# Reordering one stage of a hybrid decoder layer: page numbers read early, a norm moved, a softmax cut in two

## The chip, the core and the metric

The kernel runs on one core of one Trainium2 chip. TensorE (PE) multiplies matrices, VectorE (DVE), ScalarE (ACT) and GpSimd (POOL) work on elements, and SyncE (SP) here issues transfers only; GpSimd issues transfers too. The metric is the device time of one execution in microseconds, as the median of several runs. Less is better.

## The reference, cut to what matters

One layer is computed for a prompt group (512 tokens) and a sample group (8 sequences of 4 new tokens): a mixer of four parts side by side, then cross-attention to a memory, then a SwiGLU FFN. All weights are float32. The change touches three of the mixer's four parts.

```python
# sample attention over a paged cache: 8 sequences, 16 pages of 128 rows each
k_past = k_cache[layer, page_table].reshape(db, past, H, dh)
gate = jnp.einsum('bqhd,bnhd->bhqn', q, kmean)
_, idx = lax.top_k(gate, n_sel)                       # 3 of 8 blocks
p = jax.nn.softmax(sc, axis=-1)
o = jnp.einsum('bhqnk,bhqnkd->bhqd', p_sel, vs) + jnp.einsum('bhqk,bkhd->bhqd', p_own, own_v)
# Mamba-2 ("ssm"): chunked scan, then a gate and one norm over its 256 columns
return rms_norm(y * jax.nn.silu(z), norm_w), conv1, h1
# HGRN2 ("hgrn"): decays between any two tokens of a chunk
diff = bcum[:, :, None] - bcum[:, None, :]
att = jnp.einsum('blhk,bshk,blshk->blsh', qc, kc, dec)     # dec = exp(diff), masked
o = att applied to v, plus q * exp(bcum) times the state;  S = decayed S + k^T v
```

## The kernel before, in words

A core runs the layer as stages: inputs, the input projection (`win`), `ssm` (which also holds `hgrn`), `gdn`, and four more for the output projection, the cross-attention and the FFN. Every stage ends when TensorE, VectorE and ScalarE have all passed its end. Within a stage each engine has its own instruction list; semaphores tie them together.

The change lies in the `ssm` stage. There four pieces of work are interleaved by hand. Each is a Python generator per engine, and the string `LANES` (L2893) says whose turn it is: "m" is the main chain (`ssm_*`, then `hgrn_*`), "p" the sample attention over pages (`moba_sample_*`), "u" the L2 norms and products that prepare the next stage (`unit_*`), and "n" the norm of Mamba-2's output (`ssm_norm_*`). The same string drives all three engines, so one letter moved changes the order on each of them. Instructions of one engine run in that order; a wait holds all that stands behind it.

The main chain. When Mamba-2's states are made, VectorE gates its output `Y`, writes the squares into `xdt` and signals `tail_sq` (L1947 to L1952). `ssm_norm_tensor` (L1844) sums the squares of each half of the tokens with two matmuls into bank 4, `ssm_norm_scalar` takes the root of each half (L1968), and `ssm_norm_vector` takes the reciprocal of the 128x544 tile (L1959) and scales `Y` (L1961). HGRN2 computes its decays by halving levels, j = 1 to 7: `diff(j)` on VectorE (two subtractions into `h_d`), `exps(j)` on ScalarE (L2384), `scaled(j)` on VectorE (queries and keys times the decays), matmuls of level j on TensorE (`hgrn_tensor`), and `place(j)` on VectorE, which copies the scores of levels 0 to 4, and at the end those of 5 to 7 together, out of four rotating PSUM banks (L2303). TensorE can't reuse a bank before its scores are placed. Level j+2 is prepared while level j is multiplied. Then follow `tail_decay_vector` and the product `kd`, and with them the tail: five tiles of 128, 128, 128, 128 and 32 tokens, each with a turn step (transposes) and a product step, the last with many small matmuls for the samples.

The pages. 32 quarters (numbers 0 to 31) of keys and 32 of values (32 to 63) pass through four slots. Each quarter is four transfers of 128 KB; SP issues the even quarters, GpSimd the odd ones. The page numbers lie in a table in SBUF, so each transfer needs a number in a register (`value_load`, L439). `load_pages` reads a quarter's four numbers, waits until its slot is free, and issues its four transfers:

```python
for n in quarters:
    ...
    ids = [eng.value_load(PTAB[...]) for i in range(4)]
    m_ = n - NPG
    if 0 <= m_ < 32:
        eng.wait_ge(S("satt_turned"), 2 * m_ + 2)
    elif m_ >= 32:
        eng.wait_ge(S("ms_values_used"), m_ - 31)
```

Each number is read when the issuing queue comes to its quarter, and not before. The first four quarters of values take the slots of the last keys. Then comes the softmax: the choice of blocks ends on VectorE at L1517, nine exponentials with row sums follow on ScalarE in one step (L1553, L1554), TensorE turns the probabilities in five groups, ScalarE copies them out, and `own pv` (new tokens' values) and then `pv32` to `pv63` (one per quarter of values, four matmuls each) run on TensorE. When `pv63` is done VectorE scales the result into `ms_o` (L1525, L1526), and TensorE picks each head's rows.

Of the kernel before, what the change touches and what calls it, by code (L numbers as in the profile page):

```python
# [23 lines left out]
P = 128  # L24
# [43 lines left out]
def build(nc, a, o):  # L68
# [12 lines left out]
    with ctx:  # L81
# [226 lines left out]
        mp_stat = m(3, 16)  # L308

        NPG = 4  # L310
        pages = carve(WS, 0, NPG, 4, 2 * P)
        ms_s = carve(WS, NPG * 4 * 2 * P, PAST)
        ms_bias = carve(XN, 0, PAST + NS)
# [117 lines left out]
        def pages_sem(n):  # L431

            return S(f"pages{n % NPG}_in"), 64 * (n // NPG + 1)

        def load_pages(eng, quarters):
            for n in quarters:
                cache = a["cache_moba_k"] if n < 32 else a["cache_moba_v"]
                pg, e = divmod(n % 32, 2)
                ids = [eng.value_load(PTAB[0:1, (2 * i + e) * NPAGE + pg:(2 * i + e) * NPAGE + pg + 1], min_val=0,  # L439
                                      max_val=a["cache_moba_k"].shape[1] - 1) for i in range(4)]  # L440
                m_ = n - NPG
                if 0 <= m_ < 32:
                    eng.wait_ge(S("satt_turned"), 2 * m_ + 2)
                elif m_ >= 32:
                    eng.wait_ge(S("ms_values_used"), m_ - 31)
                else:
                    after(eng, "win")
                for i in range(4):
                    eng.dma_start(pages[:, n % NPG, i, :],  # L449
                                  cache[0].rearrange("g p h d -> g p (h d)")[bass.ds(ids[i], 1)].rearrange("g p n -> (g p) n"))\  # L450
                       .then_inc(pages_sem(n)[0], 16)
# [932 lines left out]
        def moba_sample_tensor(pe):  # L1384
# [28 lines left out]
            for j in range(66):  # L1413
# [2 lines left out]
                if j < 64:  # L1416
                    turn(j)
                yield
            for _ in range(4):
                yield  # L1420
            pe.wait_ge(S("satt_exp"), 1)
            for i in range(4):
# [65 lines left out]
        def moba_sample_vector(v):  # L1488
            moba_queries_vector(v)
            yield  # L1490
            s3 = ms_s.rearrange("p (n k) -> p n k", k=MOBA_BLOCK)
            for j in range(69):
                q, x = (j - 2) // 16 - 1, (j - 2) % 16
                if j == 8:
                    moba_rows_vector(v)
                if q >= 0 and x == 0:
                    v.wait_ge(S("ms_scores_out"), q + 2)
                    link(V.tensor_reduce(ms_gate[:, 2 * q:2 * q + 2], s3[:, 2 * q:2 * q + 2, :], AXX, ALU.add))
                elif q >= 0 and x == 1:
                    sl = slice(q * 512, (q + 1) * 512)  # L1500
                    link(V.scalar_tensor_tensor(ms_s[:, sl], ms_bias[:, sl], mr, ms_s[:, sl], ALU.mult, ALU.add))
                elif q >= 0 and x == 2:
                    link(V.tensor_reduce(ms_top[:, 2 * q:2 * q + 2], s3[:, 2 * q:2 * q + 2, :], AXX, ALU.max))
                yield
            gm = bc(ms_gate.rearrange("p (o m) -> p o m", o=1), (P, 8, 8))
            gn = bc(ms_gate.rearrange("p (n o) -> p n o", o=1), (P, 8, 8))
            link(tt(ms_gt, gm, gn, ALU.is_gt))
            link(tt(ms_eq, gm, gn, ALU.is_equal))
            link(tt(ms_eq, ms_eq, ltm, ALU.mult))
            link(tt(ms_gt, ms_gt, ms_eq, ALU.add))  # L1510
            link(V.tensor_reduce(ms_rank, ms_gt, AXX, ALU.add))
            link(V.tensor_scalar(ms_sel, ms_rank, 2.5, NEG, ALU.is_gt, ALU.mult))
            link(tt(ms_top, ms_top, ms_sel, ALU.add))
            link(V.tensor_reduce(ms_stat[:, 0:1], ms_top, AXX, ALU.max))
            link(V.tensor_reduce(ms_stat[:, 1:2], ms_own, AXX, ALU.max))
            link(V.tensor_reduce(ms_stat[:, 2:3], ms_stat[:, 0:2], AXX, ALU.max, negate=True))
            V.tensor_scalar(ms_shift, ms_sel, ms_stat[:, 2:3], None, ALU.add).then_inc(S("satt_max"), 1)  # L1517
            yield
            for _ in range(5 + 32):
                yield  # L1520
            v.wait_ge(S("satt_exp"), 1)
            link(V.tensor_reduce(ms_stat[:, 0:1], ms_sums, AXX, ALU.add))
            link(V.reciprocal(ms_stat[:, 3:4], ms_stat[:, 0:1]))
            v.wait_ge(S("ms_values_used"), 32)
            link(V.tensor_scalar(ms_o[:, 0, :], bank(7)[:, 0:GW], ms_stat[:, 3:4], None, ALU.mult))  # L1525
            V.tensor_scalar(ms_o[:, 1, :], bank(7)[:, GW:2 * GW], ms_stat[:, 3:4], None, ALU.mult).then_inc(S("satt_o"), 1)  # L1526
            yield
            yield
            v.wait_ge(S("satt_pv"), 1)
            V.tensor_copy(OM[:, 0:2, SEQ:T], bank(5)[:, 0:2 * NS].rearrange("p (c t) -> p c t", t=NS))  # L1530
            yield

        def moba_sample_scalar(s):
# [17 lines left out]
            for n in range(8):  # L1551
                sl = slice(n * MOBA_BLOCK, (n + 1) * MOBA_BLOCK)
                A.activation(ms_s[:, sl], ms_s[:, sl], ACT.Exp, bias=ms_shift[:, n:n + 1], accum_out=ms_sums[:, n:n + 1])  # L1553
            A.activation(ms_own, ms_own, ACT.Exp, bias=ms_stat[:, 2:3], accum_out=ms_sums[:, 8:9]).then_inc(S("satt_exp"), 1)  # L1554
            yield
            for i in range(4):
# [286 lines left out]

        def ssm_norm_tensor(pe):  # L1844
            pe.wait_ge(S("tail_sq"), 1)
            for j in range(2):
                if j:
                    pe.wait_ge(S("tail_root"), 1)
                for k in range(2):
                    last = mm(bank(4)[:, 0:HT], ones, half(xdt[:, k, :], j), k == 0, k == 1)  # L1850
                last.then_inc(S("tail_sum"), 1)
                yield
            yield
# [10 lines left out]
        def ssm_vector(v):  # L1864
# [84 lines left out]
                link(V.scalar_tensor_tensor(Y[:, c_, :], xc[:, c_, :], par(R_SD + c_), Y[:, c_, :], ALU.mult, ALU.add))  # L1949
            link(tt(Y, Y, proj[:, C_Z:C_Z + 2, :], ALU.mult))  # L1950
            tt(xdt, Y, Y, ALU.mult).then_inc(S("tail_sq"), 1)
            yield  # L1952

        def ssm_norm_vector(v):
# [10 lines left out]
        def ssm_norm_scalar(s):  # L1965
            for j in range(2):
                s.wait_ge(S("tail_sum"), j + 1)
                A.activation(half(rsq, j), bank(4)[:, 0:HT], ACT.Sqrt, bias=eps, scale=1.0 / GW).then_inc(S("tail_root"), 1)  # L1968
                yield
            yield  # L1970

        def ssm_scalar(s):
            def decays(i):
# [37 lines left out]
            s.dma_start(o["ssm_p"][0, 0].rearrange("(c e) q n -> (e q) c n", e=2), s_fin).then_inc(S("ssm_states_out"), 16)  # L2011
            s.wait_ge(S("states_made"), 1)
            s.dma_start(o["ssm_s"][0].rearrange("b (c e) q n -> (e q) b c n", e=2), s_h0).then_inc(S("ssm_states_out"), 16)

# [243 lines left out]
        def h_width(j):  # L2260
            return T if j < 3 else SEQ

        def hgrn_vector(v):
            v.wait_ge(S("h_k"), 1)

            def halves_of(j):
                B = 1 << j
                blocks = lambda buf: buf[:, :, 0:h_width(j)].rearrange("p c (n i) -> p c n i", i=B)
                return blocks, lambda buf: blocks(buf)[:, :, :, 0:B // 2], lambda buf: blocks(buf)[:, :, :, B // 2:B]

            def diff(j):
                B = 1 << j
                blocks, left, right = halves_of(j)
                if j > 1:
                    v.wait_ge(S("h_qk"), j - 1)
                mid = bc(blocks(h_b)[:, :, :, B // 2 - 1:B // 2], (P, 2, h_width(j) // B, B // 2))
                tt(left(h_d), mid, left(h_b), ALU.subtract)
                tt(right(h_d), right(h_b), mid, ALU.subtract).then_inc(S("h_diff"), 1)

            def scaled(j):  # L2280
                v.wait_ge(S("h_dec"), j)
                if j >= 3:
# [21 lines left out]
                return placed + len(H_JOBS[j])  # L2304

            placed = 0
            diff(1)
            link(tt(lev[:, 6, :], lev[:, 6, :], lev[:, 7, :], ALU.add))
            tt(lev[:, H_PACKED, :], lev[:, H_PACKED, :], lev[:, 6, :], ALU.add)
            scaled(1)  # L2310
            for j in range(8):
                if j + 2 < 8:
                    diff(j + 2)
                if j < H_PACKED or j == 7:
                    placed = place(j, placed)
                if j + 2 < 8:
                    scaled(j + 2)
                if j == 6:
                    v.wait_ge(S("h_lv_mm"), H_MM[6])
                    tail_decay_vector(v, 0, h_b, hq, h_q1[:, 1], h_d)  # L2320
                yield
# [57 lines left out]
            yield from tail_vector(v, 0, False, None, 4)  # L2379

        def hgrn_scalar(s):
            def exps(j):
                s.wait_ge(S("h_diff"), j)
                A.activation(h_d[:, :, 0:h_width(j)], h_d[:, :, 0:h_width(j)], ACT.Exp).then_inc(S("h_dec"), 1)  # L2384
            exps(1)
            for j in range(8):
                if j + 2 < 8:
                    exps(j + 2)
                if j == 6:
                    s.wait_ge(S("h_qk"), 7)  # L2390
                    tail_prep_scalar(s, 0, h_b, h_d)
# [494 lines left out]
        def mixer_lane(eng, ssm, hgrn):  # L2886
# [3 lines left out]
            yield from hgrn  # L2890


        LANES = "m".join(["pp"] + ["pppp"] * 14 + ["ppp"] * 3 + ["p", "p", "pn", "pn", "n"] + ["pp"] * 5  # L2893
                         + ["pppu"] * 8 + ["ppu", "pp", "pp"])

        def lanes(main, pages_, unit, norm):
            steps = {"m": main, "p": pages_, "u": unit, "n": norm}
# [148 lines left out]
```

## Time and profile before

| what | value |
|---|---|
| runs | 1511.8, 1516.27, 1517.79 us, median 1516.27 |
| the profiled execution | 1515.02 us, its span 1513.4 us |
| TensorE busy | 1349.5 us, 89% of the span |
| VectorE, ScalarE, GpSimd busy | 652.7, 476.1, 442.8 us |
| mean granted TensorE clock | 0.908 of full speed |

The profiled execution lies 1.25 us below the median of the runs. Its span is the time from the first to the last instruction; 1.6 us lie around it. Busy TensorE time counts pipelined matmuls, so it isn't work at the peak.

### The profile page before, as it was taken

How to read it: one execution, taken by the hardware profiler on the slowest of the kernel's cores; microseconds unless marked ns; L12 is line 12 of the kernel's file. 1: busy time of each engine (PE TensorE's matmuls, PEld its weight loads, DVE VectorE, ACT ScalarE, POOL GpSimd, SP SyncE). 2: the span in 40 equal slices, each digit the busy share in tenths (PEclk: the TensorE clock that was granted, in tenths of full speed). 3: DMA queues.
4: the chain of work that ended last, by engine and by line, in shares of the span. 5: the costliest groups of instructions: out<-in, count | busy, mean ns of one | idle time of the engine just before them, and what ended most of it. 6: DMA issues, size and time to landing. Idle time of an engine off the chain costs nothing.

```text
span 1513.4 us, 25049 instructions
## 1 busy us (share of the span) xinstructions
PE 1349.5 (89%) x10192; PEld 1174.3 (78%) x10192; DVE 652.7 (43%) x1088; ACT 476.1 (31%) x777; POOL 442.8 (29%) x370
## 2 busy tenths in 40 slices
PE   5998999889776797878999898989799999989999
PEld 4998987656563366778879784439799999989998
DVE  4569944243583146553243824301763333330003
ACT  3322244254143314122344432203432222222221
POOL 4424431333103402004515130003144443434330
PEclk8998999889657756988979999989999999999999
DMA  4322240456305720012424041452222232222321
GB/s 122 82 58 71 76 112 1 120 164 188 91 1 177 221 93 1 1 32 95 129 96 126 23 146 30 167 178 63 63 84 85 85 96 86 84 77 78 91 63 60
DMA packets 177556, 136.85 MB, mean 90 GB/s; under 512 B 15011, under 2 KB 165972, under 8 KB 177442
## 3 DMA queue, kind: packets, MB, share of 16 engines
q1 hardware_dynamic: 167906, 113.85, 25.3%
q0 software_dynamic: 7200, 20.23, 4.5%
q8 instruction: 80, 1.31, 0.4%
q10 hardware_dynamic: 2336, 1.18, 0.3%
q14 instruction: 34, 0.28, 0.1%
HBM read 127.27 MB, written 7.96 MB: 89 GB/s over the span
## 4 chain that ended last, share of the span: by engine, by line
PE 72%; DVE 15%; ACT 4%; issue 4%; DMA 1%; POOLq 1%; POOL 1%; SPq 0%; DVEq 0%; ACTq 0%
PE PS L258 67%; PE PS L261 6%; DVE PROJ L1733 2%; DVE SC L626 1%; POOLq L439 1%; DVE PROJ L626 1%; DVE XN L887 1%; DVE XT L626 1%; DVE XN L626 1%; POOL W_LO L242 1%; DVE PROJ L1734 1%; DVE XN_parts L878 1%; DVE RSQ L885 0%; DVE OM L1595 0%; DMA PROJ<-in_x_sample 0%
## 5 line engine op out<-in xcount | busy, mean ns | idle before, releaser
L242 POOL TENSOR_TENSOR W_LO<-W,W_HI 128x1024 fp32r<-128x1024 f32 (+1 forms) x130 | 317.8, 2448 | 799.5 <-ACT W_HI L233 799.5
L258 PE MATMUL PS<-XN_parts,W_HI 128*128 128x272 f32 x1184 | 342.5, 289 | 0.0
L258 PE MATMUL PS<-OM_parts,W_HI 128*128 128x272 f32 x960 | 277.9, 289 | 0.0
L258 PE MATMUL PS<-SC_parts,W_HI 128*128 128x272 f32 (+2 forms) x832 | 246.4, 296 | 13.1 <-POOL W_LO L242 12.2
L258 PE MATMUL PS<-SC_parts,W_LO 128*128 128x272 f32 (+2 forms) x832 | 242.6, 292 | 0.0
L258 PEld LDWEIGHTS PS<-XN_parts,W_HI 128*128 128x128 f32 x1184 | 225.2, 190 | 0.0
L258 PE MATMUL PS<-OM_parts,W_LO 128*128 128x272 f32 x704 | 203.9, 290 | 0.0
L233 ACT ACTIVATE W_HI<-W 128x1024 fp32r<-128x1024 f32 (+1 forms) x130 | 134.1, 1041 | 208.1 <-PE PS L258 208.1
L258 PEld LDWEIGHTS PS<-OM_parts,W_HI 128*128 128x128 f32 x960 | 182.1, 190 | 0.1
L258 PEld LDWEIGHTS PS<-SC_parts,W_HI 128*128 128x128 f32 x832 | 159.0, 191 | 18.3 <-POOL W_LO L242 11.2
L258 PEld LDWEIGHTS PS<-SC_parts,W_LO 128*128 128x128 f32 x832 | 158.7, 191 | 0.0
L258 PE MATMUL PS<-PROJ_parts,W_HI 128*128 128x272 f32 (+2 forms) x608 | 153.6, 294 | 5.0 <-DVEq L2884 5.0
L258 PEld LDWEIGHTS PS<-OM_parts,W_LO 128*128 128x128 f32 x704 | 132.3, 188 | 0.0
L258 PEld LDWEIGHTS PS<-PROJ_parts,W_HI 128*128 128x128 f32 x608 | 109.4, 194 | 5.4 <-DVEq L2884 5.3
L258 PE MATMUL PS<-PROJ_parts,W_LO 128*128 128x272 f32 (+2 forms) x256 | 75.9, 296 | 0.0
L449 POOL DMA_DIRECT2D W_scratch<-in_cache_moba_v x64 | 34.3, 536 | 117.7 <-PE PS L258 69.7
L258 PE MATMUL PS<-SC,XN 64*64 64x4 f32 (+3 forms) x384 | 67.4, 321 | 0.0
L626 DVE TENSOR_TENSOR SC<-SC 128x272 f32<-128x272 f32 (+6 forms) x68 | 36.5, 540 | 70.5 <-ACT SC L820 50.5
L1147 ACT ACTIVATE PROJ<-PS 128x512 f32<-128x512 f32 (+1 forms) x76 | 44.9, 597 | 55.9 <-PE PS L261 43.6
L258 PE MATMUL PS<-PROJ,XN 128*128 128x128 f32 (+3 forms) x280 | 41.8, 297 | 18.7 <-DVE XN L626 18.2
L449 POOL DMA_DIRECT2D W_scratch<-in_cache_moba_k x64 | 34.5, 539 | 81.5 <-PE PS L261 47.0
L258 PE MATMUL PS<-OM_parts,PROJ_parts 128*128 128x272 f32 x256 | 54.9, 305 | 3.7 <-DVE XN_parts L878 2.5
(374 smaller groups left out, 2260.2 us busy)
## 6 DMA issues: line engine op xcount, KB each, us to landing
W<-in_w_gu SPq DMA_DIRECT2D x44, 512.0 KB, 3.9
W<-in_w_in SPq DMA_DIRECT2D x30, 512.0 KB, 3.8
W_scratch<-in_cache_moba_k SPq DMA_DIRECT2D x64, 128.0 KB, 2.6
W_scratch<-in_cache_moba_k POOLq DMA_DIRECT2D x64, 128.0 KB, 2.7
W_scratch<-in_cache_moba_v SPq DMA_DIRECT2D x64, 128.0 KB, 2.8
W_scratch<-in_cache_moba_v POOLq DMA_DIRECT2D x64, 128.0 KB, 2.6
W<-in_w_xkv SPq DMA_DIRECT2D x16, 512.0 KB, 3.6
W<-in_w_down SPq DMA_DIRECT2D x16, 512.0 KB, 3.9
```

The lines of the kernel that those rows point to most:

```text
L233: nc.scalar.activation(hi_lo(n)[0], raw_chunk(n), ACT.Copy)\
L242: nc.gpsimd.tensor_tensor(hi_lo(n)[1], raw_chunk(n), hi_lo(n)[0].bitcast(F32), ALU.subtract).then_inc(S("weights_split"), 1)
L258: return nc.tensor.matmul(out, lhsT, rhs, start=start, stop=stop, skip_group_check=True)
L261: return nc.tensor.transpose(out, in_, ident[0:k, 0:k])
L439: ids = [eng.value_load(PTAB[0:1, (2 * i + e) * NPAGE + pg:(2 * i + e) * NPAGE + pg + 1], min_val=0, max_val=a["cache_moba_k"].shape[1] - ...
L449: eng.dma_start(pages[:, n % NPG, i, :], cache[0].rearrange("g p h d -> g p (h d)")[bass.ds(ids[i], 1)].rearrange("g p n -> (g p) n"))\
L626: return V.tensor_tensor(out, x, y, op)
L878: V.scalar_tensor_tensor(lo(k)[:, TOKENS[run][j]], XT[:, k, TOKENS[run][j]], par(GAINS[run][1] + k), hi(k)[:, TOKENS[run][j]].bitcast(F32) ...
L887: last = V.scalar_tensor_tensor(xn[:, k, c_], xn[:, k, c_], par(GAINS[run][0] + k), rsq[:, c_], ALU.mult, ALU.mult)
L1147: return A.activation(o_, i_, ACT.Copy)
L1733: V.scalar_tensor_tensor(dst[:, d:SEQ], src[:, 0:SEQ - d], wt[3 - d], dst[:, d:SEQ], ALU.mult, ALU.add)
L1734: last = V.scalar_tensor_tensor(ds_, win_[:, :, 3 - d:7 - d], wt[3 - d], ds_, ALU.mult, ALU.add)
```

## The change

It consists of five edits, all in the `ssm` stage.

1. **Page numbers.** When a queue comes to its first quarter of 36 or more, it reads the numbers of all its quarters from 36 to 59, 48 values, ahead of that quarter's wait. The four last quarters (60 to 63) are read as before.
2. **The norm.** The letters "n" move from the middle of HGRN2's levels to just before the tail's first turn step and just behind it. Its sums go to bank 2 in place of bank 4, and TensorE waits for the last `place` first.
3. **The softmax.** ScalarE's exponentials are cut behind the fifth. Between the two parts comes the main chain's step, which holds `exps(4)`. Waiting steps are counted up by one on the other engines.
4. **The first differences.** `diff(1)` runs on VectorE right behind the squares, and `exps(1)` on ScalarE at the end of Mamba-2's part.
5. **The order of the rest.** The fifth group of turned probabilities (`pt4`) and its copy come before level 5 and `exps(7)`. In the tail, quarters are spread differently: at its end the order on every engine was `u8`, tail turn, `pv63`, `ms_o`, products of the last tile, pick; it is `pv63`, `ms_o`, `u8`, tail turn, pick, products of the last tile.

```diff
+        AHEAD = 12
+        def page_ids(eng, n):
+            pg, e = divmod(n % 32, 2)
+            return [eng.value_load(PTAB[0:1, (2 * i + e) * NPAGE + pg:(2 * i + e) * NPAGE + pg + 1], min_val=0,
+                                   max_val=a["cache_moba_k"].shape[1] - 1) for i in range(4)]
         def load_pages(eng, quarters):
+            early = {}
             for n in quarters:
-                pg, e = divmod(n % 32, 2)
-                ids = [eng.value_load(...) for i in range(4)]
+                if n >= 32 + NPG and not early:
+                    early = {q: page_ids(eng, q) for q in quarters if 32 + NPG <= q < 32 + NPG + 2 * AHEAD}
+                ids = early[n] if n in early else page_ids(eng, n)
...
# moba_sample: TensorE waits 5 steps (was 4), VectorE 6 + 32 (was 5 + 32); ScalarE:
                 A.activation(ms_s[:, sl], ms_s[:, sl], ACT.Exp, bias=ms_shift[:, n:n + 1], accum_out=ms_sums[:, n:n + 1])
+                if n == 4:
+                    yield
...
         def ssm_norm_tensor(pe):
             pe.wait_ge(S("tail_sq"), 1)
+            pe.wait_ge(S("h_lv_out"), H_MM[4] + 4)
...
-                    last = mm(bank(4)[:, 0:HT], ones, half(xdt[:, k, :], j), k == 0, k == 1)
+                    last = mm(bank(2)[:, 0:HT], ones, half(xdt[:, k, :], j), k == 0, k == 1)
...
# the end of ssm_vector
             tt(xdt, Y, Y, ALU.mult).then_inc(S("tail_sq"), 1)
+            v.wait_ge(S("h_k"), 1)
+            hgrn_diff(v, 1)
...
# ssm_norm_scalar reads bank(2); the end of ssm_scalar, behind the two stores of the states
+            hgrn_exps(s, 1)
...
# hgrn_vector and hgrn_scalar: diff(1) and exps(1) left out
-        LANES = "m".join(["pp"] + ["pppp"] * 14 + ["ppp"] * 3 + ["p", "p", "pn", "pn", "n"] + ["pp"] * 5
-                         + ["pppu"] * 8 + ["ppu", "pp", "pp"])
+        LANES = "m".join(["pp"] + ["pppp"] * 14 + ["ppp"] * 3 + ["p"] * 5 + ["pp", "ppp", "pp", "pp"]
+                         + ["pppn"] + ["pppnu"] * 2 + ["pppu"] * 6 + ["ppu", "p", "p"])
```

`hgrn_diff` and `hgrn_exps` are the old inner functions `diff` and `exps` under new names.

## Rows read from the trace of the kernel before

**Rows 1.** Page: the chain that ended last, shares of the span by engine
```profile
PE 72%; DVE 15%; ACT 4%; issue 4%; DMA 1%; POOLq 1%; POOL 1%; SPq 0%; DVEq 0%; ACTq 0%
```

**Rows 2.** Busy time by stretch: length, busy by engine, PEclk, DMA share, GB/s
```profile
411.00:458.00 47.00, 29.81 (x305) 26.05 (x305) 39.90 (x70) 20.20 (x36) 0.00 (x0) 0.57 0.00 1
458.00:534.00 76.00, 55.38 (x488) 26.71 (x488) 20.66 (x46) 21.25 (x31) 30.75 (x57) 0.75 0.68 203
...
600.00:680.00 80.00, 64.49 (x554) 62.49 (x553) 45.76 (x75) 17.40 (x36) 0.00 (x0) 0.96 0.05 11
```

**Rows 3.** TensorE in time, levels to tail: start, us, instruction, [idle before <- releaser]
```profile
426.39 2.18 PE L258 MATMUL PS<-SC,CN 128*128 128x272 f32 x4
...
447.70 5.11 PE L258 MATMUL PS<-SC 64*128 64x128 f32 x32 [8.23 <-DVE PROJ L2303]
...
458.13 2.07 PE L258 MATMUL PS<-W 32*128 32x256 f32 x4 [1.99 <-ACT W L1147]
...
469.68 0.44 PE L261 MATMUL PS<-CN,SC 128*128 128x128 f32 x2 [2.55 <-DVE SC L626]
...
531.70 2.79 PE L258 MATMUL PS<-W_scratch,PROJ 128*32 128x256 f32 x24
```

**Rows 4.** VectorE in time, the levels
```profile
413.37 1.29 DVE L626 TENSOR_TENSOR SC<-PROJ,W 128x1088 f32<-128x1088 f32 x1 [0.65 <-ACT W L2384]
...
431.85 2.78 DVE L2303 COPY_PREDICATED PROJ<-CN,PS 128x512 f32<-128x512 int32 x6
...
439.32 0.69 DVE L626 TENSOR_TENSOR SC<-PROJ,W 128x512 f32<-128x512 f32 x1 [4.69 <-ACT W L2384]
...
440.53 3.54 DVE L1959 RECIPROCAL RSQ<-RSQ 128x544 f32<-128x544 f32 x1
...
445.62 1.29 DVE L626 TENSOR_TENSOR W<-PROJ 128x512 f32<-128x512 f32 x2
...
462.57 1.29 DVE L626 TENSOR_TENSOR SC<-PROJ,W 128x1088 f32<-128x1088 f32 x1 [3.33 <-PE PS L258]
```

**Rows 5.** ScalarE in time, the softmax and the norm's roots
```profile
430.77 0.51 ACT L1553 ACTIVATE W_scratch<-W_scratch,SC 128x256 f32<-128x256 f32 x1 [5.45 <-DVE SC L1517]
...
435.13 1.28 ACT L1968 ACT_TABLE_LOAD   x1
436.43 0.49 ACT L1968 ACTIVATE RSQ<-PS,CN 128x272 f32<-128x272 f32 x1
436.93 1.28 ACT L2384 ACT_TABLE_LOAD   x1
438.23 1.06 ACT L2384 ACTIVATE W<-W 128x1024 f32<-128x1024 f32 x1
...
457.83 0.25 ACT L1147 ACTIVATE W<-PS 32x128 f32<-32x128 f32 x1
```

**Rows 6.** Waits of TensorE, 404 to 555 us: us in total, times, longest
```profile
PE PS L258 <- DMA W_scratch<-in_cache_moba_v: 17.9, 8, 4.7
```

**Rows 7.** GpSimd in time: issues of the values' pages, one quarter a row
```profile
394.52 2.29 POOL L449 DMA_DIRECT2D W_scratch<-in_cache_moba_v  x4 [12.22 <-PE PS L261]
...
473.64 2.29 POOL L449 DMA_DIRECT2D W_scratch<-in_cache_moba_v  x4 [2.27 <-issue]
```

**Rows 8.** Busy time in 5 us windows of dense paging, columns as in Rows 2
```profile
290.00:295.00 5.00, 5.00 (x39) 2.70 (x37) 0.72 (x1) 1.25 (x3) 4.62 (x6) 0.57 0.88 263
```

**Rows 9.** Line L449, 458 to 535 us: from issue to landing
```profile
DMA to landing us min/median/max: 2.0/2.8/5.2
```

**Rows 10.** VectorE in time, the stage's end
```profile
532.34 0.44 DVE L626 TENSOR_TENSOR XN<-PROJ,PS 128x272 f32<-128x272 f32 x1
...
533.74 0.41 DVE L2135 COPY XN<-PS 32x256 f32<-32x256 f32 x1
...
537.30 0.48 DVE L1525 TENSOR_SCALAR W<-PS,SC 128x256 f32<-128x256 f32 x1
```

**Rows 11.** Chain of waits in time: the last tile's products
```profile
534.53 12.26 PE PS L258 x80
```

More of the change, by code:

```diff
@@ L433, in pages_sem @@
             return S(f"pages{n % NPG}_in"), 64 * (n // NPG + 1)
+        def page_ids(eng, n):
+            pg, e = divmod(n % 32, 2)
+            return [eng.value_load(PTAB[0:1, (2 * i + e) * NPAGE + pg:(2 * i + e) * NPAGE + pg + 1], min_val=0,
+                                   max_val=a["cache_moba_k"].shape[1] - 1) for i in range(4)]
         def load_pages(eng, quarters):
+            early = {}
             for n in quarters:
                 cache = a["cache_moba_k"] if n < 32 else a["cache_moba_v"]
-                pg, e = divmod(n % 32, 2)
-                ids = [eng.value_load(PTAB[0:1, (2 * i + e) * NPAGE + pg:(2 * i + e) * NPAGE + pg + 1], min_val=0,
-                                      max_val=a["cache_moba_k"].shape[1] - 1) for i in range(4)]
+                if n >= 32 + NPG and not early:
+                    early = {q: page_ids(eng, q) for q in quarters if 32 + NPG <= q < 32 + NPG + 2 * AHEAD}
+                ids = early[n] if n in early else page_ids(eng, n)
                 m_ = n - NPG
@@ L1418, in moba_sample_tensor @@
                 yield
-            for _ in range(4):
+            for _ in range(5):
                 yield
@@ L1518, in moba_sample_vector @@
             yield
-            for _ in range(5 + 32):
+            for _ in range(6 + 32):
                 yield
@@ L1967, in ssm_norm_scalar, with hgrn_exps @@
                 s.wait_ge(S("tail_sum"), j + 1)
-                A.activation(half(rsq, j), bank(4)[:, 0:HT], ACT.Sqrt, bias=eps, scale=1.0 / GW).then_inc(S("tail_root"), 1)
+                A.activation(half(rsq, j), bank(2)[:, 0:HT], ACT.Sqrt, bias=eps, scale=1.0 / GW).then_inc(S("tail_root"), 1)
                 yield
             yield
+        def hgrn_exps(s, j):
+            s.wait_ge(S("h_diff"), j)
+            A.activation(h_d[:, :, 0:h_width(j)], h_d[:, :, 0:h_width(j)], ACT.Exp).then_inc(S("h_dec"), 1)
         def ssm_scalar(s):
@@ L2261, in h_width, with halves_of, hgrn_diff @@
             return T if j < 3 else SEQ
-        def hgrn_vector(v):
[L2264 to L2278, printed above, removed]
+        def halves_of(j):
+            B = 1 << j
+            blocks = lambda buf: buf[:, :, 0:h_width(j)].rearrange("p c (n i) -> p c n i", i=B)
+            return blocks, lambda buf: blocks(buf)[:, :, :, 0:B // 2], lambda buf: blocks(buf)[:, :, :, B // 2:B]
+        def hgrn_diff(v, j):
+            B = 1 << j
+            blocks, left, right = halves_of(j)
+            if j > 1:
+                v.wait_ge(S("h_qk"), j - 1)
+            mid = bc(blocks(h_b)[:, :, :, B // 2 - 1:B // 2], (P, 2, h_width(j) // B, B // 2))
+            tt(left(h_d), mid, left(h_b), ALU.subtract)
+            tt(right(h_d), right(h_b), mid, ALU.subtract).then_inc(S("h_diff"), 1)
+        def hgrn_vector(v):
             def scaled(j):
@@ L2306, in hgrn_vector @@
             placed = 0
-            diff(1)
             link(tt(lev[:, 6, :], lev[:, 6, :], lev[:, 7, :], ALU.add))
@@ L2312, in hgrn_vector @@
                 if j + 2 < 8:
-                    diff(j + 2)
+                    hgrn_diff(v, j + 2)
                 if j < H_PACKED or j == 7:
@@ L2381, in hgrn_scalar @@
         def hgrn_scalar(s):
[L2382 to L2385, printed above, removed]
             for j in range(8):
                 if j + 2 < 8:
-                    exps(j + 2)
+                    hgrn_exps(s, j + 2)
                 if j == 6:
```

## The prediction

> **What bounds the kernel now.** I read the page's chain first: it lies on TensorE for 72% and on VectorE for 15% [rows 1], so an edit pays only where TensorE waits. Next I read busy time by stretch [rows 2]. In HGRN2's levels (411 to 458 us) TensorE is busy for 29.8 of 47 us and VectorE for 39.9: VectorE sets the pace. In the stretch of the values' pages (458 to 534 us) TensorE is busy for 55.4 of 76 us and no other engine is near full. Then I read each engine in order of time through both stretches, looking at what ends each idle time.
>
> In the levels TensorE stands 8.23 us at level 4 until scores are placed [rows 3]. They are placed late because VectorE first waits 4.69 us for `exps(4)` and then does the norm, 445.62 - 440.53 = 5.1 us [rows 4]. `exps(4)` is late because on ScalarE nine exponentials (4.36 us together, a cadence of 0.49), two table loads of 1.28 us and a root stand ahead of it, from 430.77 to 438.23 us [rows 5].
>
> In the pages' stretch TensorE waits 17.9 us in 8 pieces for value pages [rows 6]. The pages come late because they are issued late: GpSimd takes 2.29 us to issue a quarter, and 2.27 us pass before it with "issue" as the releaser, no semaphore [rows 7]. That is the reading of four page numbers. Two queues at 4.56 us a quarter give one quarter per 2.28 us, 28 quarters in 64 us.
>
> **The change part by part.** A is the moment at which TensorE starts `own pv` (458.13), B the start of the tail's first turn (469.68), C the end of `pv63` (531.70 + 2.79 = 534.5) [rows 3].
>
> *To A.* (a) `exps(1)` is made while VectorE does other work, so its wait of 0.65 us at 413.37 goes [rows 4]. (b) Only five exponentials stand ahead of `exps(4)`: it starts at about 430.77 + 5 x 0.49 = 433.2 and ends at 434.3, while VectorE places scores until 434.63 [rows 4, 5]. The wait of 4.69 us goes entirely. The softmax's second part ends 1.06 us later than it did; its reader on TensorE then still has level 3 to do, so this costs nothing. (c) The norm's 5.1 us leave this chain. After a, b and c VectorE is 10.4 us ahead. Next late is VectorE's own round (1.29 + 2.78 + 2 x 0.69 = 5.4 us [rows 4]) with TensorE's 5.11 us a level [rows 3] just behind it, so I take the whole 10.4. (d) The last probabilities' copy stood behind `exps(7)`, at 457.83 [rows 5]; now it stands before it, and `own pv` waits for level 5 alone. Level 5 needs nothing of `exps(7)` and ended before it; I estimate 1.9 us, with bounds of 1.06 (the exponential) and 2.6 (with its wait). A moves by 12.3 us, to 445.8.
>
> *To B.* VectorE's tail decay waited 3.33 us for level 6, which on TensorE stands behind `own pv`, and began 4.44 us after A (462.57) [rows 3, 4]. One more quarter now stands before level 6, 2.79 / 3 = 0.93 us [rows 3]. So it begins at 445.8 + 4.44 + 0.93 = 451.2, and B, which follows from it on VectorE, moves by as much, 11.3 us, to 458.4. TensorE's new wait for the last `place` holds the norm's first sums and the turn behind them; but the turn waits anyway for `kd`, which VectorE makes after that place, and the old wait there was 2.55 us [rows 3]. The first sums (2.18 us for both banks' passes at low clock, as at 426.39 [rows 3]) nearly fit in: 0 to 2.
>
> *From B to C.* It was 64.8 us. TensorE's own work is 64.8 - 17.9 (pages), less two quarters that now stand ahead of B (1.9), plus the second sums (2.2): 47.2 us. If pages never held it, C would be 505.6. The pages: the first wait is over once `pv32` is done, about 3 us after A, at 449. The 48 readings, at 2.27 us for four, take 27 us; GpSimd has been free since 394.52 + 2.29 = 397 [rows 7] and SP longer, so 52 us cover them. From there a quarter costs, by three bounds: by issue 2.29 / 2 = 1.15 us; by the loop of a slot, 2.29 issue + 2.8 landing [rows 9] + 0.93 for the product, 6.0 over four slots, 1.5 us; by the transfer engines 0.524 MB at 203 / 0.68 = 298 GB/s, if their share could reach one [rows 2], 1.76 us, or at the 263 GB/s of the densest window [rows 8], 2.0 us. I take 1.9, between the last two: 28 x 1.9 = 53, plus 2.8 for the landing and 2.3 for the numbers of the last quarters, gives 507. Both bounds, 505.6 and 507, are near one another, and quarters are used in threes between other steps, so that neither hides the other fully; I add 4 us: C = 511, 23.5 us earlier. The ends: 505 with nothing added, 518 at 2.15 us a quarter with the addition.
>
> The Trainium skill, in "Trainium Kernel Development and Optimization", section "Key Constraints", says that transfers from SP and GpSimd share the same 16 engines, so that issuing from several saves only issue time. By the rows issue is what is lacking now (share 0.68), so the rule doesn't forbid the gain, but caps it.
>
> VectorE's norm (5.1 us) now stands between two tail steps, beside three quarters, a unit step and a product step of TensorE (3 x 0.93 and more), and TensorE's next need of VectorE is three quarters later: 0, and up to 2 us if that cover is short. ScalarE gets one more table load, 1.28 us, in a stretch where it is busy 21 of 76 us [rows 2]: nothing.
>
> *After C.* In the old order VectorE had made `u8` (532.34 to 533.74) and the last tile's copies (0.73) when `pv63` ended, and TensorE went on at once; `ms_o` came later, beside TensorE's products [rows 10, 11]. Now `ms_o` (two of 0.48), `u8` (1.4) and the copies (0.73) follow `pv63` in a row, and the last products wait for the copies. TensorE's pick lies inside this. Cost: 3.2 us.
>
> *Sum.* 23.5 - 3.2 = 20 us less: 1515.0 - 20 = 1495 for such an execution, and 1496 against the median, which lies 1.25 us higher.
>
> A second place where page and row differ is the table load. The Trainium skill, "ScalarE: Activation LUTs", section "What ACT_TABLE_LOAD costs", gives a drain of 1.38 us beside the 1.28 us of each switch. The rows show the root starting 1.30 us behind the load's start [rows 5]; no drain is seen. By the page, the two loads taken out ahead of `exps(4)` would be worth 2.8 us more; the sum would stay, since it ends at VectorE's own work there.
>
> **The rivals.**
> - *Only the levels pay.* The transfer engines deliver hardly faster than now, because landings stretch when both queues issue without pause (a landing took up to 5.2 us [rows 9]; a loop of 2.29 + 5.2 + 0.93 over four slots is 2.1 us a quarter). C then moves by 11 to 15 us; with 3.2 off, 8 to 12: 1506. For it: a share of 0.68 already at 203 GB/s [rows 2]. Against it: the window with 263 GB/s [rows 8].
> - *The clock rises too.* The granted clock averaged 0.57 in the levels and 0.75 in the pages' stretch [rows 2], a mix of 1.2 and 2.4 GHz. With most waits gone the stretch may run at full clock; the pages still bound C at 505 to 507, and the last tile's products (12.3 us [rows 11], with a clock of a half at their start) lose up to 6. Gain 25 to 32: 1487. The Trainium skill, "TensorE: Matmul & The Clock Gate", Part 1, says that the throttled state is the default and activity releases it. The rows agree in that the sparser levels have the lower clock.
> - *The clock stays low: slower.* If small matmuls don't lift it (the window of rows 8 has TensorE busy throughout at 0.57), the stretch's work, 55.4 us at 0.75 [rows 2], is 83 at 0.5: counted from A, C is 529 and 2 us of gain are left. If it then rises later in the next stage too, whose dense part has 64.5 us of TensorE at 0.96 [rows 2], that part grows by 64.5 x (0.96 / c - 1). This decides at c = 0.92; at 0.85 it costs 8.4 us: 1521. Against it: what stood before low clocks was waiting, and that gets less.
> - *The early reading does nothing*, since the readings land behind a wait or are repeated per quarter. The gap of 2.27 us would stay and only A's gain count: 1507. The code places them ahead of the wait, so this is small.
>
> **How the numbers follow.** Forecast 1496 (1490 to 1502): 0.58. Only the levels pay, or reading in vain (1503 to 1509): 0.19. Clock up (1482 to 1489): 0.14. No change within 0.5%, 7.6 us, about what a measurement of this kernel can tell from none, by a lower clock or a wait that I haven't seen: 0.06. Slower: 0.03. The range of 8 in 10 takes in most of the two cases at its sides: 1485 to 1507. Faster by over 0.5% is everything below 1508.7: 0.90; within: 0.07; slower: 0.03.
>
> **What the profile of the changed kernel would show.** VectorE's wait before the product of level 4 is gone, and the reciprocal at L1959 stands inside the tail; `own pv` starts at about 446. GpSimd shows no "issue" gap before quarters 37 to 59; its issues start some 3.8 us apart, with TensorE as the releaser, and the transfers reach 250 to 280 GB/s from 449 to 505. TensorE's wait for the value pages falls from 17.9 to some 5 to 8 us. A new wait of about 3 us stands ahead of the last tile's products. The prediction is wrong if landings grow to 5 us, if TensorE waits in the levels for ScalarE's second softmax part, or if the gain in this stage is given back after it by a lower clock.

## The result, and the profile after

The changed kernel took 1500.45 us (median of 4 runs, 1492.76 to 1504.79) against 1515.61 for the kernel before: a ratio of 0.9897, with a 95% interval of 0.985 to 0.9944. In a later session, with 12 runs of it and 17 of the kernel before, it was 1500.37 against 1514.3, 0.9915 (0.9886 to 0.9944). So the gain is 14 to 15 us by the medians; 20 were forecast.

A single execution doesn't show this difference so exactly. The profiled one took 1492.76 us, 22 us less than the profiled one of before, but half of that isn't the change's: level 0 begins at 400.17 us in place of 405.06, after work that is the same in both, and the part behind the stage is 6.4 us shorter, again the same work. I therefore count from the first matmul of level 0 to the copy of the sample attention's output, D, the last work of VectorE that this change moves. A, B and C are those of the prediction. These markers scatter too: in the four profiles with pages, here and below, whose stretch from A to C has the changed kernel's order, it took 75.4, 73.6, 75.1 and 76.2 us.

| us behind level 0's first matmul | A (own pv) | B (first turn) | C (pv63 done) | D |
|---|---|---|---|---|
| before | 53.1 | 64.6 | 129.4 | 144.5 |
| forecast, as a shift | -12.3 | -11.3 | -23.5 | -20.3 |
| after | 39.4 | 52.7 | 114.8 | 133.5 |
| after, second profile | 39.5 | 52.4 | 113.1 | 131.8 |
| measured shifts | -13.7, -13.6 | -11.9, -12.2 | -14.6, -16.4 | -11.0, -12.8 |

The first half came as forecast, the second didn't. The levels first. ScalarE in time (start, us, instruction, idle time before it and releaser), where [rows 5] had nine exponentials, two table loads and a root ahead of `exps(4)`; L1561 is the softmax, L1987 `exps`:

```profile
424.98 0.51 ACT L1561 ACTIVATE W_scratch<-W_scratch,SC 128x256 f32<-128x256 f32 x1 [5.28 <-DVE SC L1525]
...
427.45 1.04 ACT L1987 ACTIVATE W<-W 128x1024 f32<-128x1024 f32 x1
```

`exps(4)` starts 2.47 us behind the first exponential; it was 7.46. VectorE in the same stretch goes from placing to products without a wait, where [rows 4] had 4.69 us of wait and the reciprocal, which now stands in the tail:

```profile
426.05 2.77 DVE L2319 COPY_PREDICATED PROJ<-CN,PS 128x512 f32<-128x512 int32 x6
428.74 0.67 DVE L634 TENSOR_TENSOR SC<-PROJ,W 128x512 f32<-128x512 f32 x1
...
457.88 3.55 DVE L1972 RECIPROCAL RSQ<-RSQ 128x544 f32<-128x544 f32 x1 [3.40 <-ACT RSQ L1981]
```

Then the pages. TensorE's waits from 439 to 515 us (us in total, times, longest), to be held against [rows 6]:

```profile
PE PS L258 <- DMA W_scratch<-in_cache_moba_v: 18.5, 9, 4.1
```

They were 17.9 and are 18.5. Before, all of them lay between B and C. Now 3.3 us lie ahead of B, where pages are wanted earlier, as this wait of TensorE shows, and 15.2 between B and C (14.4 in the second profile):

```profile
448.92 0.64 PE L258 MATMUL PS<-W_scratch,PROJ 128*32 128x256 f32 x8 [2.31 <-DMA W_scratch<-in_cache_moba_v]
```

Yet the numbers are read early, as planned. Line L438, the reading from the table, from 380 to 440 us, 48 times on each queue (GpSimd's are shown), and GpSimd in time:

```profile
L438 POOLq TENSOR_LOAD <-PTAB x48: 284/286/941, 391.4 to 419.4; - x48
```
```profile
454.93 4.64 POOL L457 DMA_DIRECT2D W_scratch<-in_cache_moba_v  x8 [2.41 <-PE PS L258]
462.31 2.29 POOL L457 DMA_DIRECT2D W_scratch<-in_cache_moba_v  x4 [2.74 <-PE PS L258]
```

Where a gap of 2.27 us with "issue" stood before nearly each quarter [rows 7], gaps of mostly 2 to 3 us now have TensorE as their releaser: the queue waits for a free slot, and TensorE for a page. Between the starts of quarters 37 and 63 GpSimd takes 60.7 us, 4.67 us from one of its quarters to the next, against 4.85 before; 3.8 were forecast. Busy time in windows (columns as in [rows 2]) shows the transfers in bursts, at a share of 0.90 and 0.93 in two windows and at 0.38 in the next, in which TensorE is busy without a break. Its clock is 1.00 in the first window, beside transfers at 299 GB/s; it is low in the third, behind a window in which TensorE was busy for 1.24 of 5 us:

```profile
460.00:465.00 5.00, 4.00 (x52) 2.16 (x52) 3.63 (x5) 2.00 (x4) 2.14 (x4) 1.00 0.90 299
465.00:470.00 5.00, 1.24 (x10) 0.43 (x10) 1.39 (x3) 2.87 (x4) 2.14 (x4) 0.69 0.93 306
470.00:475.00 5.00, 5.00 (x34) 2.99 (x35) 0.14 (x1) 2.97 (x5) 2.17 (x5) 0.62 0.38 127
```

Landing times of the values' pages between 438 and 516 us, against the median of 2.8 in [rows 9]:

```profile
DMA to landing us min/median/max: 2.0/3.4/5.4
```

At the stage's end stands the new wait that the prediction expected, of 2.68 us. It stands ahead of the pick, which waits for VectorE's `ms_o` and then `u8` (516.05 to 517.5). TensorE and VectorE in time:

```profile
517.66 1.04 PE L258 MATMUL PS<-CN,W 128*64 128x16 f32 x16 [2.68 <-DVE PROJ L634]
```
```profile
515.13 0.48 DVE L1533 TENSOR_SCALAR W<-PS,SC 128x256 f32<-128x256 f32 x1 [0.23 <-PE PS L258]
```

### The profile page after: what moved, and what is told of

Same layout as the page of the kernel before. It is cut to its first block, busy times and chain, and to the rows that moved or that the text cites. A ratio compares the mean times of both kernels' runs of the same rounds, so it can differ in the third digit from the quotient of the medians.

```text
span 1491.1 us, 25048 instructions
## 1 busy us (share of the span) xinstructions
PE 1332.4 (89%) x10192; PEld 1164.4 (78%) x10192; DVE 652.5 (44%) x1088; ACT 472.1 (32%) x774; POOL 442.4 (30%) x370
## 4 chain that ended last, share of the span: by engine, by line
PE 74%; DVE 15%; ACT 4%; DMA 3%; issue 2%; POOL 1%; SPq 0%; DVEq 0%; POOLq 0%; ACTq 0%
PE PS L258 68%; PE PS L261 6%; DVE PROJ L1743 2%; DMA W_scratch<-in_cache_moba_v 2%; DVE SC L634 1%; DVE PROJ L634 1%; DVE XN L895 1%; DVE XN L634 1%; DVE XT L634 1%; POOL W_LO L242 1%; DVE PROJ L1744 1%; DVE XN_parts L886 1%; DVE RSQ L893 1%; DVE OM L1605 0%; DMA PROJ<-in_x_sample 0%
## 5 line engine op out<-in xcount | busy, mean ns | idle before, releaser
L258 PEld LDWEIGHTS PS<-SC_parts,W_HI 128*128 128x128 f32 x832 | 158.5, 191 | 19.3 <-POOL W_LO L242 12.2
```

The lines of the kernel that those rows point to most:

```text
L258: return nc.tensor.matmul(out, lhsT, rhs, start=start, stop=stop, skip_group_check=True)
```

## The experiments

Two theories were left after the result. *Numbers*: the early reading is worth what was forecast, and something else took it back. *Slots*: once the numbers are there, the way from a freed slot to a landed page, with TensorE using quarters in groups of three, holds it nearly as much as before. The times are device times. Where a kernel ran only once, the verdict rests on the markers of its profile alone.

### Early numbers alone, and all but them

```diff
# only_numbers: the kernel before, with
+        def page_ids(eng, n): ...
+                    early = {q: page_ids(eng, q) for q in quarters if 32 + NPG <= q < 32 + NPG + 2 * AHEAD}
# no_numbers: the changed kernel, with
-                if n >= 32 + NPG and not early:
+                if False:
```

> The kernel before with the early reading of page numbers alone. Counted from level 0's first matmul, C (end of pv63) lies at 129.4 us in the kernel before and 114.8 in the changed one. If the early numbers are worth what the prediction says, C moves 8 to 12 us earlier, to about 119, and the whole is 0.6% faster. If slots and bursts of transfers hold TensorE instead (the theory after the first result: page waits stayed at 18.5 us), C moves by 0 to 4 us and the time can't be told from before.

> The changed kernel with page numbers read as before. If the early reading is worth 8 to 12 us, C is at 123 to 127 us behind level 0 in place of 114.8, and the kernel is 0.3% faster than before. If bursts are what holds it, C is at 115 to 119, and nearly the whole gain of the change stays.

Measured: `only_numbers` 1507.02 us against 1513.96 (10 and 25 runs), ratio 0.9967 (0.9943 to 0.999); C at 124.7, so 4.8 us earlier. `no_numbers` 1504.78, ratio 0.9956 (0.9927 to 0.9984); its A is 43.3 and its C 123.5, so A to C takes 80.2 us where the changed kernel takes 75.4 and 73.6. TensorE's page waits are 14.8 us in the first and 18.7 in the second. The C of `no_numbers` lies in the range expected for a gain of 8 to 12 us, but 3.9 us of its lag are there at A already, ahead of all pages. Counted from A, both ways give the early reading 5 to 7 us, between the two expectations. The two ratios together give 0.992, close to the whole change's 0.9915 and 0.9897: its parts add up, and nothing is seen that took the gain back. The numbers were worth about half of what was forecast. One profile each is thin ground: the D of `no_numbers` is 2.3 us earlier than that of the kernel before, where its ratio says 2 to 11 us.

The first run shows something more. Its end is in the old order, yet D - C is 12.5 us, where the kernel before has 15.1: the last products begin at the higher clock there (0.64 on average over that stretch, 0.50 before).

### Half of each page, and none

```diff
# half_pages
+                    rows_ = slice(0, 64) if n >= 32 + NPG else slice(0, 128)
-                    eng.dma_start(pages[:, n % NPG, i, :], ...
+                    eng.dma_start(pages[rows_, n % NPG, i, :], ...[rows_, :])
# no_pages: load_pages
+                if n >= 32 + NPG:
+                    continue
# and TensorE, before the products of quarter n
-                pe.wait_ge(*pages_sem(n))
+                pe.wait_ge(*pages_sem(32 + n % NPG))
```

> The changed kernel, but of each values' page from quarter 36 on only the first 64 of 128 rows are fetched, so the sample attention is computed on incomplete values; the rest is the same work. If the transfer engines' rate in bursts (300 GB/s, share 0.9 to 1) holds TensorE, its wait for value pages falls from 18.5 us to under 8 and C to about 105 us behind level 0. If the queues' issue and the way from issue to landing hold it, the wait stays above 12 us.

> The changed kernel, but the values' pages from quarter 36 on are not fetched: TensorE multiplies what the slots hold, so the sample attention is wrong, and all its other work is the same. This measures TensorE's own work from B to C, for which the prediction took 47.2 us at the old clock mix. If that term is right, C - B is 43 to 48 us; if denser work brings the full clock, it falls to 35 to 40, and pages cost more than their waits show.

Measured with half the bytes, TensorE's wait, and issue to landing:

```profile
PE PS L258 <- DMA W_scratch<-in_cache_moba_v: 12.0, 7, 2.3
```
```profile
DMA to landing us min/median/max: 2.0/2.6/3.7
```

GpSimd's four issues still take 2.27 us. So 12.0 of 17.5 to 18.5 us of wait stay when the transfer engines' share falls to 0.43: about a third goes with the bytes, and the rest doesn't. In profiles with the changed kernel's order of pages up to the end the waits scatter from 15.0 to 19.1 us, so the third is rough. From one of GpSimd's quarters to the next it takes 4.33 us (4.67 and 4.48 in the changed kernel). C - B is 56.0 us (62.1 and 60.6).

Without the transfers the stretch from A to C, in the same columns as [rows 2]:

```profile
448.11:494.51 46.40, 41.99 (x503) 24.38 (x496) 25.69 (x48) 24.48 (x34) 0.73 (x1) 0.96 0.01 3
```

It was 75.4 us for the changed kernel:

```profile
439.55:514.98 75.43, 56.69 (x504) 28.47 (x496) 26.22 (x49) 24.47 (x34) 30.77 (x57) 0.77 0.67 204
```

The same matmuls take 42.0 us of TensorE at a mean granted clock of 0.96 and 56.7 at 0.77. C - B is 33.6 us, below even the 35 to 40 expected. Pages thus cost this stretch 29.0 us. 14.7 of them are longer matmuls at the lower clock, which no row of waits shows; 14.3 are idle time. The waits for pages were 18.5, but without them TensorE stands elsewhere: 3.6 us ahead of the norm's sums, for the last `place`.

This run takes away transfers and waits together. That it is the waits that lower the clock, and not the transfers, is supported by the window at 299 GB/s above, whose clock is 1.00. Waits aren't the whole of it either: in the window of [rows 8] TensorE is busy throughout, beside 263 GB/s, and has 0.57. By how much a given wait lowers it isn't shown: `half_pages` has 12.0 us of waits, none over 2.3 us, and a clock of 0.75 from A to C, no higher than the changed kernel's.

### Groups of three quarters

```diff
# spread: the tail's rounds in LANES
-  ["pppn"] + ["pppnu"] * 2 + ["pppu"] * 6 + ["ppu", "p", "p"]
+  ["pppn"] + ["pppnu"] * 2 + ["pupp"] * 6 + ["ppu", "p", "p"]
# spread_best: also the end, and the last numbers behind the issue of quarters 44 to 47
+  ["pppn"] + ["pppnu"] * 2 + ["pupp"] * 6 + ["pu", "p", "pp"]
+                if n in (44, 45, 46, 47):
+                    early[n + 16] = page_ids(eng, n + 16)
# refill: only the last two lines
```

> The changed kernel with three edits: in six of the tail's rounds one quarter of values stands alone ahead of the unit step and two behind it (in place of three and then the unit step), the end in the old order, and the numbers of quarters 60 to 63 read in the slots' waiting time behind quarters 44 to 47. If a group of three quarters that frees its slots together is what makes TensorE wait, the wait for value pages falls from 18.5 us to 8 to 12, and the kernel is 4 to 8 us faster than the changed one. If the wait is the transfer engines' or a stop of GpSimd's queue, it stays above 14 us and only the 3 us of the end come.

> The changed kernel with the one edit of the tail's rounds: a quarter of values ahead of the unit step and two behind it. From the kernel with three edits (C 108.0 against 113 to 115) I expect that this one brings most: C 109 to 111, page waits of 15 to 17 us in more and shorter pieces, and a higher clock in the stretch (0.82 to 0.86). If the gain there came from the last quarters' numbers, C stays at 113 to 115.

> The changed kernel with the numbers of quarters 60 to 63 read behind the issue of quarters 44 to 47, where the queues wait for slots. The prediction put the late reading at 2.3 us: C at 111 to 113. If it is covered anyway, C stays at 113 to 115.

Measured in `spread_best`, waits of 16.2 us in 12 pieces, and the stretch from A to C:

```profile
443.01:511.48 68.47, 52.06 (x504) 25.50 (x496) 26.33 (x49) 24.47 (x34) 30.78 (x57) 0.85 0.74 225
```

C is at 108.0 and D at 124.8, 7 us before the changed kernel's of the same session, of which the end's order has 1.8. The waits hardly fell: they stayed above 14 us, as the rival had it, but C came 5 us earlier, which the rival hadn't. They are shorter (longest 2.3 us, was 4.1), and the clock is 0.85 in place of 0.78. `spread` alone: C at 110.1, in the range expected, but by 14.4 us of waits in 9 pieces and a clock of 0.79, so neither more and shorter pieces nor the higher clock that was expected. A to C is 70.6 us there, against 73.6 to 76.2 in four profiles with the same end, and 68.5 in `spread_best` against 71.7 in the kernel of the next section, which shares its end: the spreading is worth 3 to 6 us in the stage, by single profiles. `refill`: C at 115.5, so the last numbers were covered, and the prediction's 2.3 us for them were too many. The whole times of `spread_best` (1498.03, ratio 0.99, interval 0.9878 to 0.9923) and `spread` (1495.68, 0.9879, interval 0.9833 to 0.9924) both lie a little below the changed kernel's, and the intervals overlap: over the whole a gain isn't shown, and the 4 to 8 us expected of `spread_best` were 2.3.

### The end's order

```diff
-  ["pppu"] * 6 + ["ppu", "p", "p"]
+  ["pppu"] * 6 + ["pu", "p", "pp"]
```

> The changed kernel with the tail's end in the old order: u8 and the last tile's copies ahead of the scaling of pv63's result, the pick behind the last products. The prediction's term of 3.2 us: the time from C to the copy of the sample attention's output (D) falls from 18.7 to about 15.3 us, and VectorE's work behind pv63 no longer holds the last products. The rival: the last products wait for something else, and D - C stays at 18 or more.

Measured: D - C is 16.85 us, where it is 18.69 in the changed kernel and 15.07 before; about 15.3 was expected. TensorE's wait has another giver now, the last tile's copies:

```profile
512.82 0.39 PE L258 MATMUL PS<-PROJ,XN 32*64 32x32 f32 x2 [1.83 <-DVE XN L2169]
```

Only one quarter is left to cover VectorE's `u8` and copies; in the kernel before it was three. So half of the cost comes back. The time, 1499.32 us (0.9915, interval 0.9885 to 0.9946), isn't told apart from the changed kernel.

### Which edit moved A

```diff
# norm_back: the norm's letters among the levels, its sums in bank 4, without the new wait
-  ["p"] * 5 + ["pp", "ppp", "pp", "pp"] + ["pppn"] + ["pppnu"] * 2
+  ["p", "p", "pn", "pn", "pn"] + ["pp", "ppp", "pp", "pp"] + ["ppp"] + ["pppu"] * 2
-            pe.wait_ge(S("h_lv_out"), H_MM[4] + 4)
# softmax_whole
-                if n == 4:
-                    yield
# pt4_back
-  ["p"] * 5 + ["pp", "ppp", "pp", "pp"]
+  ["p"] * 5 + ["pp", "pp", "ppp", "pp"]
```

> The changed kernel with the norm's steps back among the levels (bank 4, no wait for the last place). By the prediction VectorE's chain gets its 5.1 us back, and exps(4) stands behind two table loads and a root again (3.0 us, of which VectorE's placing covers 0.3 to 1.3): A moves from 39.4 to about 46 to 47 us behind level 0. If TensorE was the bound behind VectorE, A moves by less than 4 us.

> The changed kernel with all nine exponentials ahead of exps(4). exps(4) then ends 1.9 us later, 1.7 us behind the end of VectorE's placing: A moves from 39.4 to 41.1. A rival: the wait is taken up at level 3's matmuls on TensorE and A stays within 0.5 us.

> The changed kernel with the fifth group of turned probabilities and its copy behind level 5 and exps(7) again. The prediction's term (d) is 1.9 us (1.06 to 2.6): A moves from 39.4 to 40.5 to 42. If the copy isn't what own pv waits for, A stays.

Measured A: 48.5, 40.9 and 42.6 us, against 39.4. The norm is worth 9.1 us, about 2 more than expected: VectorE waits 2.91 us for `exps(4)` again and then does the norm (5.1 us), 8.0 of the 9.1 us, and TensorE stands at level 4 (first line, the wait of [rows 3]). The cut of the softmax is worth 1.5 us, as expected: VectorE waits 1.49 us for `exps(4)` without it. The earlier copy of the last probabilities is worth 3.2, beyond its upper bound of 2.6; the wait for it is in the second line:

```profile
444.77 5.10 PE L258 MATMUL PS<-SC 64*128 64x128 f32 x32 [5.49 <-DVE PROJ L2318]
```
```profile
448.17 1.59 PE L258 MATMUL PS<-W 32*128 32x256 f32 x4 [3.15 <-ACT W L1155]
```

A alone has a spread that is no edit's: in `no_numbers` and `half_pages`, whose levels are those of the changed kernel, it is 43.3 and 42.7. There TensorE does its last large level at the lower clock, and VectorE's placing waits for it. The same 32 matmuls in `after` and in `no_numbers`:

```profile
434.04 2.82 PE L258 MATMUL PS<-SC 64*128 64x128 f32 x32
```
```profile
440.61 5.13 PE L258 MATMUL PS<-SC 64*128 64x128 f32 x32
```

So the prediction was right to set TensorE just behind VectorE in the levels: in two of the profiles it is TensorE that sets the pace at their end. The steps of the three kernels here don't rest on A alone, since the waits account for them.

The repeat of the changed kernel, whose second profile the table holds:

> The changed kernel once more, beside the next one on the same chip: 1.0 to 1.2% faster than before. In-stage markers, counted from level 0's first matmul: A 39 to 43 us (it depends on TensorE's clock in the levels), C 111 to 119.

The markers are in the ranges expected, A at 39.5 and C at 113.1. The ratio of 0.9915 is 0.85% faster, a little less than the 1.0 to 1.2% expected.

## Why the prediction was right, and where it missed

The sign and the size held: 1500.45 us lies in the range of 1485 to 1507, 4.4 us above the forecast. Step by step:

- *To A*, 12.3 forecast, 13.7 measured. The removed waits and the norm came in full, and VectorE's own chain was next. Term (d) was mis-sized: 1.9 forecast, 3.2 measured.
- *To B*, 11.3 forecast, 11.9 measured, but not on the path that was named. TensorE waits 3.3 us for pages on the way, a wait that the forecast had only behind B, then does the norm's first sums (450.92) and the turn right behind them (452.90). `kd` had ended at 452.0, so B lay 0.9 us behind it, within the 0 to 2 us allowed. The new wait for the last `place` cost nothing here, since the pages came later still; without pages it is 3.6 us long.
- *From B to C* is the step that failed. The forecast was 52.6 us (511 - 458.4); measured were 62.1 and 60.6, hardly under the 64.8 of before. The term that was mis-sized is the 1.9 us that a quarter costs. From quarter 37 to quarter 63 it is 60.7 / 26 = 2.34 us (2.24 in the second profile), 12 us more over 28 quarters. The 2.3 us for the last numbers came back, as `refill` shows. That leaves 10 us, and A to C took 75.4 us where 65.2 were forecast. Behind the term stand two things. The first is the way round one slot, which the sum put at 2.29 + 2.8 + 0.93 = 6.0 us and therefore left aside. In the changed kernel it is 6.6 to 9.0 us for the seven quarters of GpSimd that TensorE had to wait for (37, 41, 43, 47, 53, 55, 61), 7.7 on average. The longest of them: the slot that quarter 51 frees at about 479.4 sees its first transfer, for quarter 55, issued at 480.20, the fourth by 482.49, and TensorE takes the page at 487.38, 4.14 us late:

```profile
478.88 1.07 PE L258 MATMUL PS<-W_scratch,PROJ 128*32 128x256 f32 x16
...
487.38 1.93 PE L258 MATMUL PS<-W_scratch,PROJ 128*32 128x256 f32 x16 [4.14 <-DMA W_scratch<-in_cache_moba_v]
```
```profile
480.20 2.29 POOL L457 DMA_DIRECT2D W_scratch<-in_cache_moba_v  x4 [2.94 <-PE PS L258]
```

  That is 0.8 + 2.3 + 4.9 us and the product, 9 in place of 6. The 0.8 us from the signal to the first transfer wasn't in the sum; the landing was taken from a kernel whose queues paused between quarters. The second is the use in threes, for which 4 us were added: over four slots 7.7 us is 1.9 a quarter, so the slot's way alone doesn't make 2.34, and `spread` shortens A to C by 3 to 6 us without a faster queue. How the 10 us divide between the two isn't shown. The transfer engines' rate, from which the 1.9 had been taken, was the lesser part: `half_pages` shows two thirds of the wait standing with half the bytes.
- *The 47.2 us of TensorE's own work* came out as a sum: with the waits between B and C subtracted the changed kernel has 46.9 us (62.1 - 15.2), and 46.2 in the second profile. But it is no constant, and so was no bound: without pages B to C takes 33.6 us. The bound was the pages throughout.
- *After C*, 3.2 forecast, 18.69 - 15.07 = 3.6 measured, behind the work of VectorE that was named, though the wait stands ahead of the pick and not of the last products. Against the 12.5 us of `only_numbers`, where the old end met the higher clock, it is 6.2.
- *The rivals.* "Only the levels pay" came nearest: it had 8 to 12 us, and D moved by 11 to 13. But its mechanism isn't quite what happened. Landings did stretch (3.4 and at most 5.4 us), yet the early numbers paid 5 us. "The clock rises too" didn't come about: 0.77 against 0.75. `no_pages` shows that it does rise, to 0.96, when the pages and their waits are gone. "The early reading does nothing" is refuted by the 48 readings before 420 us and by `only_numbers`. "Slower" didn't occur. In that rival 2 us are used up at a clock of 0.93, not 0.92; nothing hangs on it.
- *Luck.* In the stage the change won 11 to 13 us of the 20 forecast, over the whole 14 to 15. No row explains the difference; the part behind D scatters by 13 us from profile to profile. So the time lies nearer to the forecast than the mechanism does.
- *The table loads.* With them gone from the levels VectorE has no wait left at level 4, whatever a load costs, so the sum ended at VectorE's own work, as said. In `norm_back`, where they are back, the root starts 1.29 us behind the start of its load, and `exps(4)` 1.29 behind the next; no drain is seen. The root's extra load in the tail is covered, since ScalarE waits 2.87 us for the sums behind it.

## What to carry to other kernels

When a gap before an issue is taken away, compute the whole way round one buffer, from the signal to the first transfer, through all its issues and the landing under load, to the use. If that is longer than the consumer's work for the buffers at hand, much of the gap only changes its name: here 2.27 us before each quarter went, and 5 to 7 of the 12 us hoped for came. Spreading the uses was worth about as much in the stage, 3 to 6 us. And a stretch with waits on TensorE can cost more than they say: here the pages' 18.5 us of waits went with 14.7 us more of the same matmuls, at a clock of 0.77 in place of 0.96.

## What wasn't expected of the hardware

GpSimd's queue stops in the midst of a quarter, in all twelve profiles with whole pages right behind the 41st transfer from quarter 37 on: for 2.75 us in four of them, the kernel before among these, for 4.2 to 5.7 us in eight, and not at all when pages are halved. In the changed kernel:

```profile
488.94 2.31 POOL L457 DMA_DIRECT2D W_scratch<-in_cache_moba_v  x4 [5.66 <-issue]
```

In each of the twelve a transfer of kind "instruction" on queue q8 runs in the stop or in the 6 us before it; `half_pages` has one there too, without a stop. That the queue waits for its own instructions, held up behind the pages, is a guess; the cause stays open. In the changed kernel the stop itself cost TensorE nothing: quarter 57, the one it cuts, was used at 496.71 without a wait, behind the products of a tile.

The same work up to level 0 took between 399.8 and 408.6 us over the 14 profiles, and the part behind D 957 to 970. A difference of 5 us can't be read from two executions' spans here, only from markers inside the stage.
